# Differential attention to its output: factors and normalisation in groups of six and two heads, the root table loaded behind the last exponentials

## The chip, the cores and the metric

The kernel runs on one core of a Trainium2 chip. The metric is the device time of one execution in microseconds; a lower number is better. The engines are TensorE (PE, matrix products), VectorE (DVE), ScalarE (ACT, activation functions), GpSimd (POOL) and SyncE (SP, here the issuer of most DMAs). Each works through its own queue in order and waits on semaphores.

## The reference, cut to what matters

The program is a chain of transformer blocks on 512 tokens of width 1024: a pooling mixer with a SwiGLU, latent attention with a SwiGLU, a norm, and then one layer of a second model, differential attention followed by a mixture of 16 experts. The change is in the differential attention. The reference computes there, for 8 heads with two score maps each:

```python
q = rmsnorm(q.reshape(B, T, H, 2, dh), q_gain) * (dh ** -0.5)
k = rmsnorm(k.reshape(B, T, H, 2, dh), k_gain)
for s in range(0, T, QBLOCK):                 # 4 blocks of 128 queries
    sc = where(dist >= 0, einsum(q, k) - slopes * dist, -inf)
    p = softmax(sc, axis=-1)
    pd = p[:, :, 0] - lam * p[:, :, 1]
    outs.append(einsum('bhqk,bkhe->bqhe', pd, v))
o = rmsnorm(concatenate(outs, axis=1), subln) * (1.0 - lambda_init)
return o.reshape(B, T, H * 2 * dh) @ w_out
```

The last norm is over the 128 values of one head and one token. Then `x = x + y`, and the experts: a router picks a group and two experts in it, for each token.

## The kernel before, in words

All activations stay in SBUF as four tiles of 128 tokens (T = 4). Weights come in units of 1 MB. Each unit is split by ACT (`split_hi`, L245) and DVE (`split_lo`, L250) into a high and a low part, and a product is three matmuls (`product`, L255 to L257).

`da_attend` walks over N = H * T = 32 blocks, a block being one head and one query tile; the order is that of one loop of each engine, with block numbers that lag behind one another. For loop number i, PE makes the scores of block i + 1 (L1642), turns block i - 6 (transposes, L1653) and weighs block i - 7 with V (L1662). DVE finds the least score of block i (L1716), every fourth time makes the head's factors (L1723, L1725), and combines the two maps of block i - 6 (L1730). ACT makes the exponentials of block i with their sums in `total` (L1686), copies the turned block i - 6 to SBUF (L1694), and at i % 4 == 3 copies the finished head i // 4 - 2 to `O` (`head_out`, L1679). The maps are not divided by their sums before the weighing: `O` is left unnormalised. POOL squares each finished head but the last and folds it to 32 columns (L1750, L1752, L1755), and DVE sums those (`sum_squares`, L1705). Head 7 is squared by DVE itself in four operations (L1741).

`da_out` then makes for all 8 heads at once the factor 1 / sqrt(mean of squares / total^2 + EPS) / total: a reciprocal and a product of `total` (L1808, L1810), times the sums of squares (L1813), plus EPS (L1815), ACT's root (L1784, for which the root table is loaded at L1782), a reciprocal (L1817) and a product (L1819). Four normalisations of 128 x 1024 follow (`normal_tile`, L1799). PE turns each normalised tile with 8 transposes (L1776), ACT rounds it to the high part (L1787), and DVE takes the low part (`lo_tile`, L1804). In DVE's queue the order is normal 0, normal 1, lo 0, normal 2, lo 1, normal 3, lo 2, lo 3. PE has the transposes of all four tiles in its queue ahead of the first product with w_out, which stands in `route` (`unit_into`) and waits for `heads_lo`.

`route` adds the products to X, makes the router's logits and tables, and stores the rows. SP issues eight units of expert weights (L1886) after the last scores were read and the last head was weighed. The other 88 (L2314) wait for the routing's count and then for a free buffer. `run_experts` takes the experts one after another.

Of the kernel before, what the change touches and what calls it, by code (L numbers as in the profile page):

```python
# [32 lines left out]
ALU = mybir.AluOpType  # L33
ACT = mybir.ActivationFunctionType
AX_X = mybir.AxisListType.X

P = 128
S = 512
T = S // P
D = 1024  # L40
C = D // P
# [8 lines left out]
H = 8  # L50
# [127 lines left out]
def build_program(nc, stream, experts, x, positions, gains, rows, lams, router, consts, band, out, moe_rows):  # L178
    ctx = ExitStack()
    with ctx:  # L180
# [1160 lines left out]
        def differential_attention(block, held, w, v, down_made, mix_row_here, mix_row, mix_rows_g):  # L1341
            QT = sb("QT", [P, H, S], where=held)
            KT = sb("KT", [P, H, S], where=held)
            V = sb("da_V", [P, T, D], where=held)
            flat = sb("da_flat", [P, 2 * T * D], where=held)
            square = sb("da_square", [P, 2, 512], where=held)
            total = sb("da_total", [P, 2, H * T], where=held)
            stat = sb("da_head_stat", [P, 2, T, H], where=held)
            ls = sb("lam_s", [P, 8], where=held)
            unsloped = sb("da_unsloped", [P, H], where=held)  # L1350
            QK = flat[:, :].rearrange("p (t n) -> p t n", t=T)
            O = flat[:, T * D:2 * T * D].rearrange("p (t d) -> p t d", t=T)
            half = flat[:, 0:T * D].rearrange("p (m n) -> p m n", m=2)
            lam_ready = sem("lam_ready")
            v_here = sem("da_emptied")
            qk_here = [sem("da_qk_emptied_act"), sem("da_qk_emptied_dve")]
            scores_read = sem("d_maxed")
            heads_out = sem("d_heads_out")
            squared = sem("d_heads_squared")

            def buffer(i, m):
                h, q = divmod(i, T)
                if q < T - 1:
                    at = 768 * (h % 2) + P * q * (q + 1) // 2
                    return half[:, m, at:at + (q + 1) * P]
                if h % 2:
                    return square[:, m, :]
                return half[:, m, 1536:2048]

            da_in(block, held, w, v, down_made, mix_row_here, mix_row, mix_rows_g, QK, V, QT, KT, square, ls, unsloped, lam_ready, v_here, qk_here)  # L1370
            scored, weighed = da_attend(block, QT, KT, V, O, buffer, total, stat, ls, held, lam_ready, v_here, qk_here,
                                        scores_read, heads_out, squared)
            made, heads_lo, _ = da_out(block, O, total, stat, heads_out, squared)
            return scored, weighed, made, heads_lo


# [231 lines left out]
        def da_attend(block, QT, KT, V, O, buffer, total, stat, ls, held, lam_ready, v_here, qk_here, maxed, heads_out,  # L1608
# [10 lines left out]
            copied = sem("d_copied")  # L1619
            weighed = sem("d_weighed")  # L1620
            head_square = sem("d_head_square")
            N = H * T
            turned_probs = sb("d_turned_probs", [P, 2, S], where=held)
            least = sb("d_least", [P, 2 * N], where=held)
# [49 lines left out]

            @block.scalar
            def _(act):
                def head_out(h):
                    act.wait_ge(weighed, T * (h + 1))
                    act.activation(head_cols(h), PS[:, 6 + h % 2, :].rearrange("p (q d) -> p q d", q=T), ACT.Copy  # L1679
# [2 lines left out]
                for i in range(N + 6):  # L1682
# [13 lines left out]
                        head_out(i // T - 2)  # L1696
                    if i == 9:
                        split_hi(act, U_DA_OUT + 1)
                head_out(H - 1)

            @block.vector
            def _(dve):
# [5 lines left out]
                for i in range(N + 6):  # L1708
# [22 lines left out]
                                                 ALU.mult, ALU.add).then_inc(combined, 1)  # L1731
                    if i == 13:
                        split_lo(dve, U_DA_OUT + 1)
                    if q == 3 and h >= 3:
                        sum_squares(h - 3)
                sum_squares(H - 2)
                dve.wait_ge(heads_out, H)
                dve.wait_ge(squared, H - 1)
                last = PS[:, 6 + (H - 1) % 2, :].rearrange("p (q d) -> p q d", q=T)
                for q in range(T):  # L1740
                    dve.tensor_tensor_reduce(head_junk[:, q, :], last[:, q, :], head_cols(H - 1)[:, q, :], 1.0, 0.0,  # L1741
                                             ALU.mult, ALU.add, stat[:, 0, q, H - 1:H]).then_inc(squared, 1)

            @block.gpsimd
            def _(pool):
# [9 lines left out]
                    pool.tensor_tensor(head_junk[:, :, 0:32], head_junk[:, :, 0:32], head_junk[:, :, 32:64],  # L1755
                                       ALU.add).then_inc(head_square, 1)

            return scored, weighed


        def da_out(block, O, total, stat, heads_out, squared):
            made = sem("do_made")
            step = sem("do_step")
            rooted = sem("do_rooted")
            normal = sem("do_normal")
            heads_turned = sem("do_turned")
            heads_hi = sem("do_hi")
            heads_lo = sem("do_lo")
# [1 line left out]

            @block.tensor
            def _(pe):
                for t in range(T):
                    pe.wait_ge(normal, t + 1)
                    for c in range(C):
                        mm = pe.transpose(PS[:, 2 * t + c // 4, (c % 4) * P:(c % 4 + 1) * P],  # L1776
                                          O[:, t, c * P:(c + 1) * P], ident)
                    mm.then_inc(heads_turned, 1)

            @block.scalar  # L1780
            def _(act):
                act.activation(spare[:, 3:4], ident[:, 0:1], ACT.Sqrt).then_inc(rooted, 1)  # L1782
                act.wait_ge(step, 5)
                act.activation(stat[:, 1, :, :], stat[:, 0, :, :], ACT.Sqrt).then_inc(rooted, 1)  # L1784
                for t in range(T):
                    act.wait_ge(heads_turned, t + 1)
                    act.activation(AH[:, :, t * P:(t + 1) * P], tile_banks(t), ACT.Copy,  # L1787
# [3 lines left out]

            @block.vector
            def _(dve):
                inverse = total[:, 1, :].rearrange("p (h q) -> p q h", q=T)
                first = total[:, 0, :].rearrange("p (h q) -> p q h", q=T)

                def normal_tile(t):
                    o = O[:, t, :].rearrange("p (h d) -> p h d", h=H)
                    dve.tensor_tensor(o, o, stat[:, 1, t, :].unsqueeze(2).broadcast_to([P, H, P]),  # L1799
                                      ALU.mult).then_inc(normal, 1)  # L1800

                def lo_tile(t):
                    dve.wait_ge(heads_hi, t + 1)
                    dve.scalar_tensor_tensor(AL[:, :, t * P:(t + 1) * P], tile_banks(t), gain_col("da_sub"),  # L1804
                                             AH[:, :, t * P:(t + 1) * P].bitcast(F32), ALU.mult,
                                             ALU.subtract).then_inc(heads_lo, 1)

                dve.reciprocal(inverse, first).then_inc(step, 1)  # L1808
                dve.wait_ge(step, 1)
                dve.scalar_tensor_tensor(first, inverse, 1.0 / P, inverse, ALU.mult, ALU.mult).then_inc(step, 1)  # L1810
                dve.wait_ge(step, 2)
                dve.wait_ge(squared, H - 1 + T)
                dve.tensor_tensor(stat[:, 0, :, :], stat[:, 0, :, :], first, ALU.mult).then_inc(step, 1)  # L1813
                dve.wait_ge(step, 3)
                dve.tensor_scalar(stat[:, 0, :, :], stat[:, 0, :, :], EPS, None, ALU.add).then_inc(step, 2)  # L1815
                dve.wait_ge(rooted, 2)
                dve.reciprocal(stat[:, 0, :, :], stat[:, 1, :, :]).then_inc(step, 1)  # L1817
                dve.wait_ge(step, 6)
                dve.tensor_tensor(stat[:, 1, :, :], stat[:, 0, :, :], inverse, ALU.mult).then_inc(step, 1)  # L1819
                dve.wait_ge(step, 7)  # L1820
                normal_tile(0)
                normal_tile(1)
                lo_tile(0)
                normal_tile(2)
                lo_tile(1)
                normal_tile(3)
                lo_tile(2)
                lo_tile(3)
                for d in range(2, 4):
# [803 lines left out]
```

## Time and profile before

| | before |
|---|---|
| median of 3 runs | 1577.47 us |
| lowest and highest | 1574.33 and 1578.65 us |
| the profiled execution's own time | 1572.86 us |
| its span | 1571.0 us |
| mean granted clock of TensorE | 0.979 |
| PE busy | 1505.6 us, 96% |
| DVE busy | 779.9 us, 50% |
| ACT busy | 674.1 us, 43% |
| POOL busy | 78.9 us, 5% |

The profile is of one execution; times in it are microseconds from the start of its span. Busy shares are means over the whole span; what ends a wait in one stage is read from that stage. The granted clock is a share of 2.4 GHz: 1.00 is 2.4 GHz, 0.50 is 1.2 GHz. A line such as L255 can be that of a helper that many stages use.

### The profile page before, as it was taken

What the parts mean: (1) busy time and instruction counts of PE and PEld (TensorE: products, weight loads), DVE (VectorE), ACT (ScalarE), POOL (GpSimd) and SP (SyncE); (2) the same over time, 40 slices, a digit from 0 to 9 for tenths busy, and PEclk for the clock granted to TensorE, in tenths of its full rate; (3) what the DMA queues carried; (4) which work ended last, traced back from release to release, by engine and by line L of the source; (5) the groups of instructions that cost most, each with busy time, mean ns of one, the idle gap of its engine ahead of it and who ended that gap; (6) DMA issues with size and microseconds to landing.
All of it is one profiled execution on the core that took longest, in us unless ns stands there. A gap on an engine that the chain in (4) does not pass through costs nothing.

```text
span 1571.0 us, 19018 instructions
## 1 busy us (share of the span) xinstructions
PE 1505.6 (96%) x7399; PEld 1245.2 (79%) x7399; DVE 779.9 (50%) x941; ACT 674.1 (43%) x853; POOL 78.9 (5%) x57
## 2 busy tenths in 40 slices
PE   8899999999899999999999999999889789999996
PEld 8888888888787788888888887788557678888874
DVE  6433323232566335232332216335773679898884
ACT  5322222212355424222222124433772368777773
POOL 0000000000000000000000000000130012111210
PEclk9999999999999999999999999999998889999998
DMA  6123222232230032322223232232131379999993
GB/s 242 60 101 107 82 105 92 96 107 94 81 108 28 8 114 81 107 83 103 100 87 108 92 109 81 98 107 81 57 140 76 144 276 383 384 394 395 382 381 87
DMA packets 36207, 226.18 MB, mean 144 GB/s; under 512 B 5271, under 2 KB 5527, under 8 KB 11824
## 3 DMA queue, kind: packets, MB, share of 16 engines
q1 hardware_dynamic: 31392, 212.06, 35.9%
q0 software_dynamic: 4608, 13.22, 3.6%
q8 instruction: 45, 0.74, 0.2%
q14 instruction: 18, 0.15, 0.0%
q10 hardware_dynamic: 144, 0.03, 0.0%
HBM read 215.22 MB, written 13.63 MB: 146 GB/s over the span
## 4 chain that ended last, share of the span: by engine, by line
PE 53%; DVE 5%; DMA 3%; ACT 2%; issue 2%; DVEq 0%; ACTq 0%; SPq 0%; POOLq 0%
PE PS L255 16%; PE PS L257 16%; PE PS L256 16%; DMA eraw<-experts 3%; PE PS L1642 1%; PE PS L1662 1%; ACT WEH L2399 1%; PE PS L2332 1%; PE PS L1653 1%; DVE da_flat L1716 1%; DVE WL L250 1%; DVE WEL L2461 1%; PE PS L1982 1%; PE PS L1453 0%; PE PS L2355 0%
## 5 line engine op out<-in xcount | busy, mean ns | idle before, releaser
L250 DVE TENSOR_TENSOR WL<-raw,WH 128x2048 fp32r<-128x2048 f32 x93 | 214.0, 2301 | 432.8 <-ACT WH L245 432.8
L255 PE MATMUL PS<-AH,WL 128*128 128x512 f32 (+1 forms) x768 | 286.7, 373 | 4.3 <-DVE AL L303 4.3
L256 PE MATMUL PS<-AL,WH 128*128 128x512 f32 (+1 forms) x768 | 286.0, 372 | 0.0
L257 PE MATMUL PS<-AH,WH 128*128 128x512 f32 (+1 forms) x768 | 285.9, 372 | 0.0
L245 ACT ACTIVATE WH<-raw 128x2048 fp32r<-128x2048 f32 x93 | 177.6, 1910 | 241.2 <-PE PS L257 241.2
L2461 DVE TENSOR_TENSOR WEL<-eraw,WEH 128x2048 fp32r<-128x2048 f32 x96 | 217.3, 2287 | 21.7 <-ACT WEH L2399 21.4
L2399 ACT ACTIVATE WEH<-eraw 128x2048 fp32r<-128x2048 f32 x96 | 182.4, 1915 | 35.1 <-DMA eraw<-experts 24.5
L255 PEld LDWEIGHTS PS<-AH,WL 128*128 128x128 f32 x768 | 145.6, 190 | 29.7 <-DVE AL L303 4.5
L257 PEld LDWEIGHTS PS<-AH,WH 128*128 128x128 f32 x768 | 145.5, 189 | 25.0
L256 PEld LDWEIGHTS PS<-AL,WH 128*128 128x128 f32 x768 | 145.6, 190 | 24.8
L255 PE MATMUL PS<-WH,AL 128*128 128x512 f32 (+2 forms) x416 | 156.3, 376 | 7.7 <-DVE WL L250 7.7
L257 PE MATMUL PS<-WH,AH 128*128 128x512 f32 (+2 forms) x416 | 154.2, 371 | 0.0
L256 PE MATMUL PS<-WL,AH 128*128 128x512 f32 (+2 forms) x416 | 153.8, 370 | 0.0
L255 PE MATMUL PS<-WEH,AH 128*128 128x512 f32 x256 | 102.4, 400 | 5.7 <-DVE AH L2466 5.5
L257 PE MATMUL PS<-WEH,AH 128*128 128x512 f32 x256 | 100.4, 392 | 0.0
L256 PE MATMUL PS<-WEL,AH 128*128 128x512 f32 x256 | 100.3, 392 | 0.0
L255 PEld LDWEIGHTS PS<-WH,AL 128*128 128x128 f32 x416 | 79.4, 191 | 21.6 <-DVE WL L250 6.9
L257 PEld LDWEIGHTS PS<-WH,AH 128*128 128x128 f32 x416 | 79.3, 191 | 12.9
L256 PEld LDWEIGHTS PS<-WL,AH 128*128 128x128 f32 x416 | 79.3, 191 | 12.2
L255 PE MATMUL PS<-WH,f0FL 128*128 128x512 f32 x176 | 69.8, 396 | 0.0
L257 PE MATMUL PS<-WH,f0FH 128*128 128x512 f32 x176 | 69.6, 395 | 0.0
L256 PE MATMUL PS<-WL,f0FH 128*128 128x512 f32 x176 | 69.6, 395 | 0.0
(317 smaller groups left out, 2112.7 us busy)
## 6 DMA issues: line engine op xcount, KB each, us to landing
eraw<-experts SPq DMA_DIRECT2D x96, 1024.0 KB, 15.6
raw<-stream SPq DMA_DIRECT2D x94, 1024.0 KB, 4.8
out<-X SPq DMA_DIRECT2D x5, 512.0 KB, 2.7
moe_rows<-moe_rows_g SPq DMA_DIRECT2D x5, 512.0 KB, 2.7
X<-x SPq DMA_DIRECT2D x4, 512.0 KB, 5.4
ffn_row<-rows SPq DMA_DIRECT2D x2, 512.0 KB, 9.2
final_row<-rows SPq DMA_DIRECT2D x2, 512.0 KB, 5.9
cst<-consts SPq DMA_DIRECT2D x1, 739.5 KB, 13.6
```

The costliest lines, as they stand in the source:

```text
L245: act.activation(WH[:, u % SLOTS, :], raw[:, u % SLOTS, :], ACT.Copy).then_inc(unit_hi, 1)
L250: dve.tensor_tensor(WL[:, u % SLOTS, :], raw[:, u % SLOTS, :], WH[:, u % SLOTS, :].bitcast(F32), ALU.subtract).then_inc(unit_lo, 1)
L255: pe.matmul(acc, lhs_lo, rhs_hi, start=start, stop=False)
L256: pe.matmul(acc, lhs_hi, rhs_lo, start=False, stop=False)
L257: return pe.matmul(acc, lhs_hi, rhs_hi, start=False, stop=stop)
L1642: pe.matmul(PS[:, 2 * (i % 2) + m, 0:(q + 1) * P], QT[rows64, h, q * P:(q + 1) * P], KT[rows64, h, 0:(q + 1) * P], start=True, stop=True). ...
L1653: mm = pe.transpose(PS[:, 4 + j % 2, k * P:(k + 1) * P], buffer(j, 0)[:, k * P:(k + 1) * P], ident)
L1662: mm = pe.matmul(PS[:, 6 + h % 2, q * P:(q + 1) * P], turned_probs[:, j % 2, k * P:(k + 1) * P], V[:, k, h * P:(h + 1) * P], start=(k == 0 ...
L1716: dve.tensor_tensor_reduce(buffer(i, m), PS[:, 2 * (i % 2) + m, 0:w], const("alibi")[:, S - w:S], 2.0 ** (-8.0 * (h + 1) / H), -NEG * 1e8, ...
L1982: mm = pe.matmul(PS[:, 2 * t, 0:20], m.XT[:, t, c, :], m.wr[:, c, :], start=(c == 0), stop=(c == C - 1))
L2399: act.activation(WEH[:, k % ESLOTS, :], eraw[:, k % ERAW, :], ACT.Copy).then_inc(unit_hi, 1)
L2461: dve.tensor_tensor(WEL[:, k % ESLOTS, :], eraw[:, k % ERAW, :], WEH[:, k % ESLOTS, :].bitcast(F32), ALU.subtract).then_inc(unit_lo, 1)
```

## The change

The factors are made in two parts: heads 0 to 5 (`PARTS[0]`), and heads 6 and 7 (`PARTS[1]`). All of it moves from `da_out` into `da_attend`.

- On DVE the two operations on `total` stand in the loop at i = 35, behind combine 29. Behind the loop come the mean square of part 0, its factors, and the normalisation of tiles 0 and 1 for part 0, all ahead of the row sum of head 6 and the squares of head 7. Behind those come part 1's factors and the other six normalisations.
- The addition of EPS is dropped; it is the bias of ACT's root.
- On ACT the dummy root, which brings the table load, stands in the loop at i = 33, the root of part 0 at i = 36 (ahead of the copy of block 31), and the root of part 1 behind the copy out of head 7.
- PE's transposes are in eight groups, of 6 or 2 columns blocks, in the order of the normalisations. The first product still stands behind all of them.
- In `da_out` DVE has only the four `lo_tile` left.

```diff
@@ da_attend, scalar
+                def head_root(act, part):
+                    act.wait_ge(stepped, 3 + 2 * part)
+                    act.activation(stat[:, 1, :, PARTS[part]], stat[:, 0, :, PARTS[part]], ACT.Sqrt, bias=const("eps")
+                                   ).then_inc(rooted, 1)
...
+                    if i == N + 1:
+                        act.activation(spare[:, 3:4], ident[:, 0:1], ACT.Sqrt).then_inc(rooted, 1)
+                    if i == N + 4:
+                        head_root(act, 0)
                 head_out(H - 1)
+                head_root(act, 1)
@@ da_attend, vector
+                    if i == N + 3:
+                        dve.reciprocal(inverse, first).then_inc(stepped, 1)
+                        dve.wait_ge(stepped, 1)
+                        dve.scalar_tensor_tensor(first, inverse, 1.0 / P, inverse, ALU.mult, ALU.mult).then_inc(stepped, 1)
                     if q == 3 and h >= 3:
                         sum_squares(h - 3)
+
+                def mean_square(part):
+                    mine = PARTS[part]
+                    dve.wait_ge(stepped, 2 + 2 * part)
+                    dve.wait_ge(squared, H - 1 + T if part else H - 2)
+                    dve.tensor_tensor(stat[:, 0, :, mine], stat[:, 0, :, mine], first[:, :, mine], ALU.mult
+                                      ).then_inc(stepped, 1)
+
+                def factors(part):
+                    mine = PARTS[part]
+                    dve.wait_ge(rooted, 2 + part)
+                    dve.reciprocal(stat[:, 0, :, mine], stat[:, 1, :, mine]).then_inc(stepped, 1)
+                    dve.wait_ge(stepped, 4 + 2 * part)
+                    dve.tensor_tensor(stat[:, 1, :, mine], stat[:, 0, :, mine], inverse[:, :, mine], ALU.mult
+                                      ).then_inc(factored, 1)
+                    dve.wait_ge(factored, 2 * H + 1 + part)
+
+                def normal_part(t, part):
+                    o = O[:, t, :].rearrange("p (h d) -> p h d", h=H)[:, PARTS[part], :]
+                    size = PARTS[part].stop - PARTS[part].start
+                    dve.tensor_tensor(o, o, stat[:, 1, t, PARTS[part]].unsqueeze(2).broadcast_to([P, size, P]),
+                                      ALU.mult).then_inc(normal, 1)
+
+                mean_square(0)
+                factors(0)
+                normal_part(0, 0)
+                normal_part(1, 0)
                 sum_squares(H - 2)
...
                 # four squares of head 7
+                mean_square(1)
+                normal_part(2, 0)
+                factors(1)
+                normal_part(0, 1)
+                normal_part(1, 1)
+                normal_part(3, 0)
+                normal_part(2, 1)
+                normal_part(3, 1)
@@ da_out, tensor
-                for t in range(T):
-                    pe.wait_ge(normal, t + 1)
-                    for c in range(C):
+                for n, (t, part) in enumerate(((0, 0), (1, 0), (2, 0), (0, 1), (1, 1), (3, 0), (2, 1), (3, 1))):
+                    pe.wait_ge(normal, n + 1)
+                    for c in ((6, 7) if part else range(6)):
                         mm = pe.transpose(PS[:, 2 * t + c // 4, (c % 4) * P:(c % 4 + 1) * P],
                                           O[:, t, c * P:(c + 1) * P], ident)
-                    mm.then_inc(heads_turned, 1)
+                    if part:
+                        mm.then_inc(heads_turned, 1)
```

## Rows read from the trace of the kernel before

**Rows 1.** The page's part 4, the chain by engine, shares of the span.

```profile
PE 53%; DVE 5%; DMA 3%; ACT 2%; issue 2%; DVEq 0%; ACTq 0%; SPq 0%; POOLq 0%
```

**Rows 2.** The chain in order of time: start us, length us, what.

```profile
1173.56 0.61 ACT da_flat L1679
...
1458.52 18.95 DMA eraw<-experts
```

**Rows 3.** Timeline of PE: start, length, line, operation, count, idle before and releaser.

```profile
1186.34 1.84 PE L1776 MATMUL PS<-cst,da_flat 128*128 128x128 f32 x8 [0.36 <-DVE da_flat L1799]
1187.93 0.48 PE L255 MATMUL PS<-WH,AL 128*128 128x512 f32 x1
```

**Rows 4.** Windows: stretch, its length, busy by engine, PEclk, DMA share, GB/s.

```profile
1174.00:1178.00 4.00, 0.00 (x0) 0.00 (x0) 3.27 (x15) 1.87 (x4) 0.00 (x0) 0.96 1.01 375
1178.00:1184.00 6.00, 3.68 (x16) 3.28 (x16) 3.93 (x5) 2.23 (x2) 0.00 (x0) 0.50 1.01 423
1184.00:1188.00 4.00, 3.63 (x17) 3.23 (x17) 3.12 (x3) 1.11 (x1) 0.00 (x0) 0.51 0.31 129
1280.00:1450.00 170.00, 170.00 (x810) 141.37 (x810) 152.90 (x88) 135.28 (x96) 35.07 (x18) 1.00 1.01 385
```

**Rows 5.** Timeline of SP, the issues of expert weights.

```profile
1163.31 12.29 SPq L1886 DMA_DIRECT2D eraw<-experts  x8
...
1263.25 263.61 SPq L2314 DMA_DIRECT2D eraw<-experts  x88
```

**Rows 6.** Timeline of DVE, combines 30 and 31, squares, factors, normalisation, low parts.

```profile
1169.35 0.60 DVE L1730 SCALAR_TENSOR_TENSOR da_flat<-da_flat,d_factor 128x384 f32<-128x384 f32 x1
1169.88 0.74 DVE L1730 SCALAR_TENSOR_TENSOR da_square<-da_square,d_factor 128x512 f32<-128x512 f32 x1
...
1174.19 0.29 DVE L1741 CUSTOM_DVE_ANT_0 d_head_junk<-PS,da_flat 128x128 f32<-128x128 f32 x1 [0.45 <-ACT da_flat L1679]
...
1175.04 0.35 DVE L1808 RECIPROCAL da_total<-da_total 128x32 f32<-128x32 f32 x1
...
1177.11 2.36 DVE L1799 TENSOR_TENSOR da_flat<-da_flat,da_head_stat 128x1024 f32<-128x1024 f32 x2
1181.54 1.28 DVE L1804 SCALAR_TENSOR_TENSOR AL<-PS,gain,AH 128x1024 fp32r<-128x1024 f32 x1 [2.07 <-ACT AH L1787]
1182.74 1.22 DVE L1799 TENSOR_TENSOR da_flat<-da_flat,da_head_stat 128x1024 f32<-128x1024 f32 x1
```

**Rows 7.** Timeline of ACT's copies and table load, and of PE behind the copies.

```profile
1167.34 0.60 ACT L1694 ACTIVATE d_turned_probs<-PS 128x512 f32<-128x512 f32 x1 [0.39 <-PE PS L1653]
1168.98 0.28 ACT L1694 ACTIVATE d_turned_probs<-PS 128x128 f32<-128x128 f32 x1 [1.05 <-PE PS L1653]
1169.89 0.39 PE L1662 MATMUL PS<-da_V,d_turned_probs 128*128 128x128 f32 x2
...
1174.18 1.28 ACT L1782 ACT_TABLE_LOAD   x1
1175.47 0.20 ACT L1782 ACTIVATE spare<-cst 128x1 f32<-128x1 f32 x1
```

**Rows 8.** Timeline of DVE's factor operation without and with POOL beside it.

```profile
1162.16 0.22 DVE L1725 SCALAR_TENSOR_TENSOR d_factor<-d_factor,lam_s,da_total 128x4 f32<-128x4 f32 x1
...
1166.57 1.04 POOL L1750 TENSOR_TENSOR d_head_junk<-da_flat 128x512 f32<-128x512 f32 x1 [4.64 <-ACT da_flat L1679]
1166.60 1.03 DVE L1725 SCALAR_TENSOR_TENSOR d_factor<-d_factor,lam_s,da_total 128x4 f32<-128x4 f32 x1
...
1171.04 1.04 POOL L1750 TENSOR_TENSOR d_head_junk<-da_flat 128x512 f32<-128x512 f32 x1 [2.09 <-ACT da_flat L1679]
```

**Rows 9.** Windows of other stretches, for the granted clock (columns as in rows 4).

```profile
966.00:970.00 4.00, 4.00 (x12) 3.15 (x11) 4.00 (x3) 2.78 (x6) 0.00 (x0) 0.57 0.78 266
1132.00:1134.00 2.00, 0.17 (x2) 0.00 (x0) 1.93 (x9) 1.13 (x4) 1.41 (x2) 1.00 0.48 70
1243.00:1269.00 26.00, 13.06 (x53) 11.82 (x53) 17.24 (x53) 12.29 (x12) 4.19 (x3) 0.50 0.40 145
```

More of the change, by code:

```diff
@@ L1370, in differential_attention @@
             da_in(block, held, w, v, down_made, mix_row_here, mix_row, mix_rows_g, QK, V, QT, KT, square, ls, unsloped, lam_ready, v_here, qk_here)
-            scored, weighed = da_attend(block, QT, KT, V, O, buffer, total, stat, ls, held, lam_ready, v_here, qk_here,
+            scored, weighed, normal = da_attend(block, QT, KT, V, O, buffer, total, stat, ls, held, lam_ready, v_here, qk_here,
                                         scores_read, heads_out, squared)
-            made, heads_lo, _ = da_out(block, O, total, stat, heads_out, squared)
+            made, heads_lo, _ = da_out(block, O, normal)
             return scored, weighed, made, heads_lo
@@ L1621, in da_attend @@
             head_square = sem("d_head_square")
+            stepped = sem("d_stat_step")
+            rooted = sem("d_rooted")
+            normal = sem("d_normal")
+            PARTS = (slice(0, H - 2), slice(H - 2, H))
+            inverse = total[:, 1, :].rearrange("p (h q) -> p q h", q=T)
+            first = total[:, 0, :].rearrange("p (h q) -> p q h", q=T)
             N = H * T
@@ L1756, in _, with da_out @@
                                        ALU.add).then_inc(head_square, 1)
-            return scored, weighed
-        def da_out(block, O, total, stat, heads_out, squared):
+            return scored, weighed, normal
+        def da_out(block, O, normal):
             made = sem("do_made")
-            step = sem("do_step")
-            rooted = sem("do_rooted")
-            normal = sem("do_normal")
             heads_turned = sem("do_turned")
@@ L1772, in _ @@
             def _(pe):
-                for t in range(T):
-                    pe.wait_ge(normal, t + 1)
-                    for c in range(C):
+                for n, (t, part) in enumerate(((0, 0), (1, 0), (2, 0), (0, 1), (1, 1), (3, 0), (2, 1), (3, 1))):
+                    pe.wait_ge(normal, n + 1)
+                    for c in ((6, 7) if part else range(6)):
                         mm = pe.transpose(PS[:, 2 * t + c // 4, (c % 4) * P:(c % 4 + 1) * P],
                                           O[:, t, c * P:(c + 1) * P], ident)
-                    mm.then_inc(heads_turned, 1)
+                    if part:
+                        mm.then_inc(heads_turned, 1)
             @block.scalar
             def _(act):
-                act.activation(spare[:, 3:4], ident[:, 0:1], ACT.Sqrt).then_inc(rooted, 1)
-                act.wait_ge(step, 5)
-                act.activation(stat[:, 1, :, :], stat[:, 0, :, :], ACT.Sqrt).then_inc(rooted, 1)
                 for t in range(T):
@@ L1793, in _ @@
             def _(dve):
[L1794 to L1800, printed above, removed]
                 def lo_tile(t):
@@ L1806, in lo_tile @@
                                              ALU.subtract).then_inc(heads_lo, 1)
[L1808 to L1822, printed above, removed]
                 lo_tile(0)
-                normal_tile(2)
                 lo_tile(1)
-                normal_tile(3)
                 lo_tile(2)
```

## The prediction

> **What bounds the kernel now.** I read the page's chain first, by engine: TensorE (PE) holds 53% of the span and every other engine a few per cent [rows 1], so a change on VectorE (DVE) counts only where PE stands still for it. The chain in order of time shows where: the last head's weighed sum is copied out from 1173.56 [rows 2], and the first product with w_out starts at 1187.93 [rows 3]. In these 14.4 us single steps of DVE, ScalarE (ACT) and PE take turns: squares of head 7, factor steps to 1177.11, then tile by tile normalise, transpose, round, take the rest. PE has all four tiles' transposes ahead of the first product, so the last normalisation and its eight transposes (from 1186.34, 1.84 us) stand in series before it.
>
> The windows add the clock [rows 4]: 0.96 on average in 1174 to 1178, where PE does nothing, and 0.50 (1.2 GHz) until just before the products; a transpose then takes 0.23 us.
>
> What follows shifts as a block. The expert weights have eight buffers, filled by eight issues from 1163.31; the other 88 issues start at 1263.25 [rows 5], behind the routing, which is behind these products. From there the DMA is busy all the time (share 1.01, 385 GB/s, [rows 4]), and the end of the chain waits for it, 18.95 us in one piece [rows 2]. A stream that starts x earlier ends x earlier, and nothing of it can start before the routing has counted its rounds. So a microsecond saved ahead of 1187.93 is worth one at the end.
>
> **The change, step by step.** I take the times of the profiled run and play the new order of each queue against them.
>
> (a) Two small operations on `total`, a reciprocal (0.35) and the product of inverses (as 1162.16, 0.22), move in front of the row sum of head 5 and combines 30 and 31, at i = 35 on DVE [rows 6, 8]. Combine 30 (1169.35, 0.60) then ends at 1170.5 instead of 1169.95, combine 31 at 1171.2. PE turned block 30 right behind the matmuls of 1169.89 [rows 7], at about 1170.3; now it can't before 1170.55. I charge 0.3 us on the attention's last blocks.
>
> (b) The root table load goes to ACT at i = 33, behind the copy that starts at 1167.34 and ends at 1167.94. It costs 1.28 and its dummy root 0.20 [rows 7]. The copy for block 28 starts at 1169.4 instead of 1168.98 and ends at 1169.7; PE needs it for the matmuls of 1169.89. Hidden, with 0.2 to spare, at no cost; with that cover gone it costs up to 1.5. The Trainium skill, page "ScalarE: Activation LUTs", section "What ACT_TABLE_LOAD costs", adds some 1.38 us of drain to a load of 1.28; by it the copy would end at 1171.1 and the last head come about 1.1 us later than in my sum. The trace disagrees: the load at 1174.18 starts 0.02 behind the copy before it, and its own activation 1.29 later.
>
> (c) `head_root(0)` stands on ACT ahead of copy 31 and waits for DVE's mean square of heads 0 to 5. Behind it are queued copy 31, for which PE's last weighed sum waits, and head 7's copy out, for which DVE's squares wait. The mean square comes behind combine 31 (1171.2), just when GpSimd (POOL) squares head 6 (1171.04, 1.04 us). What that can do is in [rows 8]: DVE's factor operation takes 0.22 at 1162.16, and 1.03 at 1166.60 beside the same POOL square. Both read two SBUF tiles, as the mean square does. Bounds: nothing, if POOL's square is the one that waits, to 1.0 us. I take that POOL goes first: mean square ends 1172.25, root 1172.5, copy 31 ends 1173.1, the last sum 1174.3, and head 7 is in SBUF at 1174.95 instead of 1174.16: 0.8 later, the 0.3 of (a) included.
>
> (d) Meanwhile DVE does factors(0) and two normalisations of six heads. A tile of 1024 columns takes 1.14 from start to start (2.36 for two, less the last one's 1.22), and 384 columns take 0.60 where 1024 take 1.22 [rows 6]: 0.97 ns a column, so 768 columns cost 0.89 and 256 columns 0.39. Reciprocal and product (0.47), and at most 0.3 of waiting for each of POOL's last two operations, put the first normalisation at 1173.4 and the end of the second at 1175.2. With the row sum of head 6 it is 1175.4. Head 7 has been there since 1174.95: from here DVE is the chain.
>
> (e) From 1175.4 DVE does: four squares, 0.85 (1174.19 to 1175.04); mean square 0.25; tile 2 of six heads 0.89, under which ACT's second root disappears; reciprocal and product 0.47; two tiles of two heads 0.79; tile 3 of six 0.89; two of two 0.79. That is 4.93, to 1180.3. Then the first lo tile, 1.20 start to start (1181.54 to 1182.74), to 1181.5. Its inputs are there: the last transposes of tile 0 go at about 1178.4, and ACT's rounding (1.1) is over by 1179.9. Product at 1181.55. The other lo tiles end 1.2 apart and PE takes 12 x 0.227 = 2.7 a tile, so they are hidden. Eight normalisations instead of four cost 4 x 0.08 = 0.3, in that sum; the addition of EPS is gone into the root's bias.
>
> (f) Clock. PE no longer stands still for 4.9 us; its longest gap is some 1.3. But behind 1174.3 it has only 12 transposes (1.3 us at full clock) in three microseconds. Rows for both sides [rows 9]: 1.00 in 1132 to 1134 with PE busy 0.17 of 2; 0.57 in 966 to 970 with PE busy throughout. If the clock falls near 1177.7, the remaining 20 transposes take 4.6 us, the first product starts at 1182.3, and PE works without a break before it, as from 1184 on, where the clock then rose. Bounds: nothing; 0.7 if it rises before the products; 2.4 if 3.4 us of products run cold (4 us at a mean of 0.57 are 3.4 us at 0.50), half of which is lost. I take 0.3, between the first two.
>
> Sum: 1187.93 - 1181.55 = 6.4, less 0.3 is 6.1; 6.0 with a few new semaphore waits of some 0.03. The ends are 7.4 (POOL waits, no clock loss) and 4.0. The profiled run took 1572.86 us with a span of 1571.0, so it would take 1566.9. The median of the timed runs is 1577.47, 4.6 above that run; for the median I forecast 1571.5.
>
> **Rivals.**
> 1. The clock falls and the products start cold: 0.7 + 1.7, gain 4.0, time 1573.5. For it: products did run cold in 966 to 970 [rows 9], and six-head bursts are thin work. Against it: 1184 to 1188 [rows 4], where PE had little but sixteen transposes, and the mean of 0.51 is 0.50 with the rise at the very end, just before the first product. The Trainium skill, page "TensorE: Matmul & The Clock Gate", Part 4 "PE-mode transpose", says that transposes don't count as PE-busy; by it the clock would fall and rise well inside the products, which is this rival. The trace speaks against the rule with that 0.51. 25%.
> 2. ACT's new load and root hold up the last blocks more than I charge: copy 28 misses its slot, or the mean square waits for all of POOL's three operations (to 1173.4). Head 7 comes at 1176.3 and DVE waits 0.9 for it: gain 5.1, with both 4.5; time 1572.7. For it: 1.03 instead of 0.22 [rows 8]. Against it: POOL's three wait for one another, and DVE can go in between. 10%.
> 3. The block doesn't shift whole: the thin work of the routing meets the clock otherwise, or the expert stream gives the time back. For it: 26 us of the routing at 0.50 [rows 9], so the clock there is at the edge. Against it: the stream is the end, and starts from the routing alone. Gain 1, time 1576.5. 8%.
> 4. Slower: the clock falls at about 1177.7 and stays at 1.2 GHz under the products, as it stayed in 1243 to 1269 [rows 9]. A product matmul then takes twice its 0.227, so half of the cold time is lost; the gain of 6.4 is gone after 12.8 us of it, and with 20 us the kernel is 3.6 slower, 1581. Against it: PE works without a break there, as from 966 on, where most of the 4 us were cold but not all. 4%.
>
> **Numbers.** Forecast 53%, with 1570 to 1573.2 as its own range; rivals 25, 10, 8 and 4%. A measurement of this kernel can tell about 0.3% (4.7 us) from no change. The forecast (gain 5 to 7.4, and medians spread a microsecond or so) gives faster in some 0.85 of its cases, rival 1 in a third, rival 2 in half, which with rounding is 0.60; 0.05 slower, the rest the same. The range takes in rivals 1 and 2 and, with a microsecond of spread, both ends of the sum, and leaves out the last two: 1568 to 1576.
>
> **What would show it.** In the changed kernel's trace: the first product at 1181 to 1182.5, and the 88 issues from about 1257; the table load behind block 27's copy, and block 28's copy still ahead of its matmuls; head 7's copy out at about 1174.4, because ACT's root waited for a mean square as long as POOL's square; DVE without a gap from head 6's row sum to the first lo tile; the clock low under transposes at most. I am wrong if the products start after 1183, if DVE waits for head 7, if products run at 0.43 each, or if the stream's start moves and the end doesn't.

## The result, and the profile after

The changed kernel took 1566.38 us (median of 5 runs, 1565.85 to 1571.12). The kernel before took 1574.83 us in the same measurement (median of 5, 1574.33 to 1578.65). The ratio is 0.9948, with a 95% interval of 0.9928 to 0.9968: faster by half a per cent, 8.2 us. Forecast were 1571.5 us and a gain of 6.0. The time is 5.1 us below the forecast and 1.6 us below its stated range; the gain was forecast 2.2 us smaller than this measurement has it.

Two more measurements of the changed kernel, described below, gave ratios of 0.9958 and 0.9949. Over all three, 21 runs of it have a mean of 1568.3 us; 83 runs of the kernel before, in three later measurements, have one of 1575.6 (standard deviation of a single run 2.3 and 3.4). The difference is 7.3 us, with some 1.2 us of uncertainty from the spread of the runs; how far measurements differ beyond that is shown below. One execution of a version below (late table) took 3868.05 us, at a clock of 1.00, and is left out of its mean and ratio.

The profiled execution took 1566.38 us, with a span of 1564.6. PE in order of time (start, length, line, operation, count, idle before; L1828 is the old L1776):

```profile
1173.62 0.88 PE L1828 MATMUL PS<-cst,da_flat 128*128 128x128 f32 x6
1174.76 0.87 PE L1828 MATMUL PS<-cst,da_flat 128*128 128x128 f32 x6 [0.26 <-DVE da_flat L1776]
1177.17 4.10 PE L1828 MATMUL PS<-cst,da_flat 128*128 128x128 f32 x20 [1.54 <-DVE da_flat L1776]
1181.54 0.47 PE L255 MATMUL PS<-WH,AL 128*128 128x512 f32 x1 [0.27 <-DVE AL L1846]
```

The last line is the number the forecast turned on: the first product starts at 1181.54, where it started at 1187.93 [rows 3] and 1181.55 was worked out before the clock's 0.3. This trace reached the stage 0.21 earlier than the one before did (combine of block 28 at 1167.45 against 1167.66); without that it is 1181.75, against 1181.95 with the clock and the semaphore waits in. DVE, and then ACT, in the same stretch:

```profile
1170.17 0.74 DVE L1746 SCALAR_TENSOR_TENSOR da_square<-da_square,d_factor 128x512 f32<-128x512 f32 x1
1170.84 0.19 DVE L1761 TENSOR_TENSOR da_head_stat<-da_head_stat,da_total 128x24 f32<-128x24 f32 x1
1172.19 2.51 DVE L1776 TENSOR_TENSOR da_flat<-da_flat,da_head_stat 128x768 f32<-128x768 f32 x2
1175.04 0.29 DVE L1788 CUSTOM_DVE_ANT_0 d_head_junk<-PS,da_flat 128x128 f32<-128x128 f32 x1
1177.47 2.30 DVE L1776 TENSOR_TENSOR da_flat<-da_flat,da_head_stat 128x256 f32<-128x256 f32 x5
1180.11 4.86 DVE L1846 SCALAR_TENSOR_TENSOR AL<-PS,gain,AH 128x1024 fp32r<-128x1024 f32 x4 [0.34 <-ACT AH L1837]
```

```profile
1167.74 1.28 ACT L1711 ACT_TABLE_LOAD   x1
1169.03 0.20 ACT L1711 ACTIVATE spare<-cst 128x1 f32<-128x1 f32 x1
1169.14 0.26 ACT L1705 ACTIVATE d_turned_probs<-PS 128x128 f32<-128x128 f32 x1
1173.62 0.60 ACT L1690 ACTIVATE da_flat<-PS 128x512 f32<-128x512 f32 x1 [1.25 <-PE PS L1668]
```

The mean square (1170.84) takes 0.19 and not 1.0. The two normalisations ahead of head 7's squares (1172.19) take 2.51 together, the five behind them (1177.47) run without a gap, and lo tile 0 waits 0.34 for ACT. The table load (1167.74) holds up block 28's copy: against [rows 7] that starts 0.16 later, in a trace that is 0.21 earlier as a whole, so by 0.37. The matmuls that read it still start in their old place, 0.21 earlier (1169.68 for 1169.89): the delay is hidden.

The windows (columns as in rows 4) and SP's issues:

```profile
1174.00:1178.00 4.00, 2.20 (x16) 1.73 (x15) 3.68 (x16) 0.52 (x2) 0.00 (x0) 0.93 0.93 363
1178.00:1181.00 3.00, 3.00 (x17) 2.80 (x15) 2.66 (x5) 2.04 (x2) 0.00 (x0) 0.52 1.01 410
1181.00:1184.00 3.00, 2.73 (x14) 2.10 (x13) 3.00 (x4) 2.20 (x3) 0.00 (x0) 1.00 1.02 429
1280.00:1450.00 170.00, 170.00 (x808) 141.45 (x808) 153.75 (x88) 136.73 (x97) 35.91 (x19) 1.00 1.02 389
```

```profile
1163.10 13.13 SPq L1911 DMA_DIRECT2D eraw<-experts  x8
1257.50 264.16 SPq L2339 DMA_DIRECT2D eraw<-experts  x88
```

The clock fell near 1177.4 and was back ahead of the products. The stream of the 88 issues starts 5.75 us earlier than in [rows 5]: 0.64 of the 6.4 went in the routing. Its thin matmuls (PE waits for DVE, then 32 of 20 columns) stand in the chain of waits after with

```profile
1234.02 5.23 PE PS L2007 x32
...
1471.66 19.02 DMA eraw<-experts
```

where the chain of the kernel before, in the same place, has

```profile
1240.39 4.61 PE PS L1982 x32
```

The low clock reaches more of them now: 0.50 on average in 1236 to 1240 here, 1.00 in the same window of before and 0.57 in 1242 to 1246, where the same matmuls stand there. The stream, from its first issue to the end of the span, took 307.10 us instead of 307.75 and gave that back. The sum, before less after: 0.21 ahead of block 28's combine, -0.27 in the last blocks, 6.45 from head 7's copy out to the first product, -0.64 in the routing, 0.65 in the stream, together 6.4. The last term is chance: the stream took 304.9 to 311.0 us in the 13 traces of this document, and 307.0 to 309.6 in the three of the changed kernel.

### The profile page after: what moved, and what is told of

It reads as the page before. It is cut to its first block, busy times and chain, and to the rows that moved or that the text cites. A ratio compares the mean times of both kernels' runs of the same rounds, so it can differ in the third digit from the quotient of the medians.

```text
span 1564.6 us, 19025 instructions
## 1 busy us (share of the span) xinstructions
PE 1504.3 (96%) x7399; PEld 1244.3 (80%) x7399; DVE 780.5 (50%) x947; ACT 673.8 (43%) x854; POOL 79.5 (5%) x57
## 4 chain that ended last, share of the span: by engine, by line
PE 53%; DVE 5%; DMA 3%; issue 2%; ACT 2%; DVEq 0%; ACTq 0%; SPq 0%; POOLq 0%
PE PS L255 16%; PE PS L257 16%; PE PS L256 16%; DMA eraw<-experts 3%; PE PS L1648 1%; PE PS L2357 1%; DVE da_flat L1732 1%; PE PS L1659 1%; DVE WL L250 1%; PE PS L2007 1%; ACT WEH L2424 1%; PE PS L1668 1%; PE PS L1453 0%; DVE da_flat L1746 0%; DVE WEL L2486 0%
```

## The experiments

All were run on one core; each measurement of several kernels shares its runs of the kernel before. Since the 13 traces reach this stage up to 4 us apart (below), the stage is read by the distance between two of its own events: from the start of head 7's copy out to the first product, 14.37 us before (1173.56 to 1187.93) and 7.92 after (1173.62 to 1181.54).

The second column is from one trace of each version. Where a kernel was traced more than once, it came to 14.37 and 14.31 (before), and to 7.92, 7.49 and 8.11 (change); so a difference under 0.6 between two versions means something only where the clock did the same in both. The means are over 12, 8, 12, 12, 12, 6, 11, 8, 8, 6 and 8 runs, from the top. Diffs are cut to the lines that matter, and `@@` names the engine.

| kernel | copy out to product, us | ratio to before, 95% interval | mean of its runs, us |
|---|---|---|---|
| before, again | 14.31 | 1.0023 (1.0006 to 1.0041) | 1578.1 |
| change, again | 7.49 | 0.9958 (0.9941 to 0.9974) | 1568.8 |
| order only | 11.12 | 0.9987 (0.9973 to 1.0001) | 1572.8 |
| early steps | 13.68 | 0.9991 (0.9976 to 1.0005) | 1574.8 |
| before, PE filled | 12.77 | 0.9994 (0.9977 to 1.0011) | 1573.3 |
| change, no POOL on head 6 | 6.81 | 0.9939 (0.9920 to 0.9958) | 1565.7 |
| change, late table | 11.81 | 0.9985 (0.9971 to 0.9999) | 1573.2 |
| change, tile first | 8.11 | 0.9955 (0.9938 to 0.9971) | 1568.7 |
| all three remedies | 6.59 | 0.9956 (0.9938 to 0.9973) | 1567.8 |
| change, PE filled | 7.48 | 0.9945 (0.9927 to 0.9964) | 1566.8 |
| change, third time | 8.11 | 0.9949 (0.9929 to 0.9970) | 1568.0 |

The kernel before against itself gave 1.0023, an interval that leaves out 1. A ratio here is thus no better than 0.2 to 0.3%, and differences between two versions are read from the second column.

### Both kernels again

No edit.

> The kernel before, unchanged, to see how its executions spread. The change gained 6.4 us between two profiled executions but 8.4 us between medians. Theory C (clock): executions differ in when TensorE's clock falls and rises, so a run with a mean granted clock lower by 0.002 has some 6 us more at 1.2 GHz and takes 2 to 4 us longer; the profiled execution of before (1572.86 us, clock 0.979) had the clock back just at its first product, at 1187.9, and most others have it back later. Then the runs here spread over 1573 to 1579 in a few steps, and the first product of this trace runs partly at 0.43 us a matmul. Rival N (chance): the runs spread evenly with no tie to the clock, and the first product starts at 1187.9 at full clock again, with a time near 1575.

> The changed kernel, unchanged, beside the one before on the same chip. Theory C: again 8 us (ratio 0.9948, +-0.001) between the medians, and the first product at 1181.5 with a full clock, because the clock's low stretch is over under the transposes whatever its position. Rival N: the 8.4 was chance; the ratio comes to 0.9960 (6.4 us).

The runs of the kernel before spread over 1571 to 1584, and those beside them over 1569 to 1580. Longer runs go with a lower mean clock: of the 83, the 13 with 0.980 have a mean of 1571.5, the 20 with 0.979 one of 1573.3, the 14 with 0.978 1575.2, and the 17 with 0.976 1578.5; of the 21 of the changed kernel, those with 0.982 1566.6 and those with 0.979 1570.5. The other part of theory C fell: in the second trace of before the first product ran at full clock too. The changed kernel's second ratio, 0.9958, is what rival N said (0.9960), but its interval takes in theory C's 0.9948 too. The spread comes from elsewhere, ahead of this stage and behind it, in code that no version here changed. The windows of the kernel before [rows 9] have 0.57 in 966 to 970; those of the changed kernel, second time:

```profile
962.00:966.00 4.00, 2.10 (x10) 1.44 (x9) 3.96 (x4) 2.59 (x4) 0.00 (x0) 1.00 0.08 16
966.00:970.00 4.00, 4.00 (x19) 3.32 (x18) 3.96 (x5) 2.78 (x6) 0.00 (x0) 1.00 0.69 250
```

What that is worth is seen between two reciprocals of the same code. DVE in the kernel before:

```profile
958.33 0.16 DVE L277 RECIPROCAL rstd<-rstd 128x1 f32<-128x1 f32 x1 [1.55 <-ACT rstd L708]
...
979.00 0.16 DVE L277 RECIPROCAL rstd<-rstd 128x1 f32<-128x1 f32 x1
```

and in the changed kernel, second time:

```profile
957.66 0.16 DVE L277 RECIPROCAL rstd<-rstd 128x1 f32<-128x1 f32 x1 [1.54 <-ACT rstd L708]
...
976.73 0.16 DVE L277 RECIPROCAL rstd<-rstd 128x1 f32<-128x1 f32 x1
```

20.67 us against 19.07: one low stretch costs 1.6 us here. The same execution of the changed kernel then had a low stretch where the one before had none:

```profile
1132.00:1136.00 4.00, 2.06 (x18) 1.61 (x16) 3.90 (x15) 2.83 (x8) 1.41 (x2) 1.00 0.69 223
1132.00:1136.00 4.00, 4.00 (x21) 2.92 (x20) 2.40 (x11) 3.04 (x10) 0.38 (x1) 0.57 0.61 240
```

The first is the kernel before; between two reciprocals around it DVE took 14.01 us there (1133.24 to 1147.25) and 15.78 in the second (1130.74 to 1146.52), so the 1.6 were lost again. Block 28's combine started anywhere from 1166.70 to 1170.72 in the 13 traces, with hardly a difference in the code before it.

### The order alone, and the early steps alone

```diff
                 normal_tile(0)
                 normal_tile(1)
-                lo_tile(0)
                 normal_tile(2)
-                lo_tile(1)
                 normal_tile(3)
+                lo_tile(0)
+                lo_tile(1)
                 lo_tile(2)
```

> The kernel before with one thing changed: in DVE's queue the four normalisations stand ahead of the four lo tiles; no groups, nothing earlier. Theory A (the order is most of it): the normalisations end at 1181.8, PE has its last transposes done by 1184.4, lo tile 0 ends at 1183; the first product starts near 1184.4 instead of 1187.9, 3.5 us or more of the change's 6.4. Theory B (the work done ahead of the last head is most of it): PE's cold transposes (0.23 each, 32 of them from 1178.4) or the lo tiles hold it up, and the product starts at 1186 or later, under 2 us of gain.

The product came 11.12 us behind the copy out, 3.2 us earlier than before: theory A, with 3.5 expected. The four normalisations run on, and PE turns all four tiles in one piece of 6.54 us at 0.2 us each; PE, mostly at 1.2 GHz (0.50 in 1178 to 1181), is the limit, since the product follows its last transpose at once and lo tile 0 was over at 1181.96:

```profile
1177.42 6.54 PE L1776 MATMUL PS<-cst,da_flat 128*128 128x128 f32 x32 [4.86 <-DVE da_flat L1799]
1183.71 0.48 PE L255 MATMUL PS<-WH,AL 128*128 128x512 f32 x1
```

The second kernel keeps the table load, the two operations on `total` and EPS where the change puts them, but makes one group of 8 heads, in the old queues. The lines of DVE are told in words here.

```diff
                 head_out(H - 1)
-                head_root(act, 1)
+                act.activation(stat[:, 1, :, :], stat[:, 0, :, :], ACT.Sqrt, bias=const("eps"))
@@ vector: no parts; behind the squares of head 7
+                tensor_tensor, reciprocal, tensor_tensor on all 8 heads
+                normal_tile(0), normal_tile(1), lo_tile(0), normal_tile(2), ...
```

> The changed kernel without its groups: the table load at i = 33, the two operations on total at i = 35 and EPS in the root's bias stay, but the factors are made for all 8 heads at once behind the last squares, and the queues of DVE and PE are as before (normal 0, 1, lo 0, normal 2, lo 1, ...). Theory A and B both: 0.35 + 0.2 + 0.3 us are gone from the chain, 0.3 comes back from the later combines; the first normalisation starts at 1176.5 instead of 1177.1 and the first product at 1187.3, 0.6 us of gain. Rival T (the table load behind the last exponentials matters): 1.3 us or more.

13.68, 0.7 earlier than before, 0.6 expected. Rival T fell: with one group, ACT's table load was no part of the chain, and moving it alone is worth little.

### What the early table load is worth

```diff
-                    if i == N + 1:
-                        act.activation(spare[:, 3:4], ident[:, 0:1], ACT.Sqrt).then_inc(rooted, 1)
-                    if i == N + 4:
-                        head_root(act, 0)
                 head_out(H - 1)
+                act.activation(spare[:, 3:4], ident[:, 0:1], ACT.Sqrt).then_inc(rooted, 1)
+                head_root(act, 0)
```

> The changed kernel with the root table loaded where it was before, behind head 7's copy out, and the root of part 0 behind it; groups and orders stay. It measures what the early load is worth. Theory: the root of part 0 is over at 1.49 + 0.6 + 0.3 = 2.4 us behind the start of head 7's copy, the two normalisations that stood ahead of the squares come behind that, and the first product is 1.8 (two normalisations) + 2.4 - 1.0 later: 10.5 to 11 us behind head 7's copy out instead of 7.9, so the early load carries some 3 us of the gain. Rival: DVE's chain has slack, and the product comes less than 1.5 us later.

11.81, 3.9 later than with the change and 0.8 more than the 10.5 to 11 expected; lo tile 0 waited 0.56 for ACT (0.34 in the changed kernel), beside transposes at 1.2 GHz (0.50 in 1184 to 1188). DVE, with the mean square of part 0 long done, waits 4.94 us for the root, and everything of head 7 stands behind it:

```profile
1174.10 0.21 DVE L1759 TENSOR_TENSOR da_head_stat<-da_head_stat,da_total 128x24 f32<-128x24 f32 x1
1179.24 0.30 DVE L1765 RECIPROCAL da_head_stat<-da_head_stat 128x24 f32<-128x24 f32 x1 [4.94 <-ACT da_head_stat L1685]
1179.82 1.83 DVE L1774 TENSOR_TENSOR da_flat<-da_flat,da_head_stat 128x768 f32<-128x768 f32 x2
```

So the early load carries all that the groups bring: with a late one the kernel comes out 0.7 behind the order alone (11.12), by one trace of each. And without the groups the load is worth nothing that shows (13.68). The two normalisations take 1.83 here, where POOL is idle.

### POOL beside the first normalisations

```diff
-                sum_squares(H - 2)
+                dve.tensor_reduce(stat[:, 0, :, H - 2], head_junk[:, :, 0:32], AX_X, ALU.add).then_inc(squared, 1)
@@ gpsimd
-                for h in range(H - 1):
+                for h in range(H - 2):
```

> The changed kernel without POOL's three operations on head 6, so head 6's sums of squares are left out (the row sum is still taken, of old data). It measures what POOL costs DVE in the new place. Theory L (two engines, one way to SBUF): the two six-head normalisations of tiles 0 and 1 take 1.8 together instead of 2.5, the row sum follows at once, and the mean square and everything else of DVE up to the squares of head 7 is 0.7 to 0.9 earlier; but head 7's copy out is the limit then, so the first product is 0.4 to 0.8 us earlier, 7.1 us behind the copy. Rival: the 2.5 us are the normalisation's own, and nothing moves.

This kernel leaves out head 6's squares, so it is a measurement and no version to use. As theory L had it: DVE's pair takes 1.83 instead of 2.51, and the product comes at 6.81 instead of 7.49, in two traces with the clock at 1.00. The pair in this kernel, and POOL in the changed one:

```profile
1171.68 1.83 DVE L1776 TENSOR_TENSOR da_flat<-da_flat,da_head_stat 128x768 f32<-128x768 f32 x2
```

```profile
1170.83 1.10 POOL L1805 TENSOR_TENSOR d_head_junk<-da_flat 128x512 f32<-128x512 f32 x1 [2.10 <-ACT da_flat L1690]
1172.01 0.74 POOL L1807 TENSOR_TENSOR d_head_junk<-d_head_junk 128x256 f32<-128x256 f32 x1
1172.83 1.05 POOL L1810 TENSOR_TENSOR d_head_junk<-d_head_junk 128x128 f32<-128x128 f32 x1
```

POOL's last operation, 0.45 alone, takes 1.05 too: each waits for the other in turn. The Trainium skill, page "SBUF — State Buffer", section "Who interferes with whom", says that a VectorE instruction with two SBUF inputs contends with a GpSimd instruction that reads SBUF, and that the port pair they share is an exclusive lock; the 0.68 and the 0.60 agree.

### The low clock

Matmuls that nobody reads keep PE at work in its gaps: in the kernel before 19 behind the last weighed sum and 9 ahead of tile 2, in the changed one 5 behind the transposes of tile 1's first six heads.

```diff
+                def keep_busy(bank, count):
+                    for _ in range(count):
+                        pe.matmul(PS[:, bank, :], WH[:, u0 % SLOTS, 0:P], WH[:, u0 % SLOTS, 0:512], start=True, stop=True)
+                pe.wait_ge(unit_lo, u0 + 2)
+                keep_busy(3, 19)
                 for t in range(T):
+                    if t == 2:
+                        keep_busy(7, 9)
                     pe.wait_ge(normal, t + 1)
```

> The kernel before, with PE kept at work in its two gaps: 19 matmuls of 512 columns into a free PSUM bank behind the last weighed sum, and 9 ahead of tile 2's transposes; nobody reads them. It measures what the low clock cost before. Theory C: the clock stays 1.00 through 1174 to 1190, transposes take 0.11 us instead of 0.23, the first product comes 12.5 us behind head 7's copy out instead of 14.35 (two times 0.9 us on the chain), and the timed runs, whose clock is 0.977 in the mean against 0.979 of the profiled one, gain more than that: 3 us or more, with mean clocks of 0.981 and above. Rival N (the spread is not from here): the trace gains 1.8 us and the timed runs gain 1.8 too, with the spread as before.

> The changed kernel with the five filling matmuls alone. In one profiled execution of the changed kernel the clock fell under the transposes and the first product came 7.92 us behind head 7's copy out, in another it did not and it came 7.49. Theory: the fill makes it 7.5 every time, 0.4 us at most. Rival: the five matmuls delay the transposes of tile 2, and it is 7.9 or later.

Before: 12.77, 1.5 to 1.6 earlier, and the windows show 1.00 throughout:

```profile
1174.00:1178.00 4.00, 4.00 (x22) 3.46 (x23) 2.11 (x13) 2.29 (x4) 0.90 (x2) 1.00 1.00 360
1178.00:1184.00 6.00, 5.42 (x32) 4.15 (x30) 4.68 (x6) 2.25 (x3) 0.00 (x0) 1.00 1.00 415
```

The timed runs gained 2.1 us in the mean, with a standard error of 1.1 (the ratio, 0.9994, has about 1). That doesn't tell theory C's 3 from rival N's 1.8. The mean clock rose from 0.978 to 0.981, some 10 us less at 1.2 GHz, for 1.5 to 1.6 us of this stage: only the transposes that ACT and DVE waited for lengthen it. After: 7.48, as in the trace in which the clock stayed up by itself (7.49). The fill cost nothing in that trace; by the traces in which the clock fell (7.92 and 8.11) it can be worth 0.4 to 0.6, but with one trace it isn't shown that it was the fill that kept the clock up.

### Toward a better version

First only the order. In DVE's queue lo tile 0 stands ahead of normal(2, 1) and lo tile 1 ahead of normal(3, 1); PE's transposes of these two stand behind the first products of tile 0 and of tile 1.

```diff
                 lo_tile(0)
+                normal_part(dve, 2, 1)
                 lo_tile(1)
+                normal_part(dve, 3, 1)
@@ route, tensor
                         mm = unit_into(d, t)
+                        if d == 0 and t < 2:
+                            turn_late(pe, 6 + t)
```

> The changed kernel, with lo tile 0 ahead of the last two normalisations of two heads in DVE's queue, and PE's transposes of those behind the first product of tile 0 and of tile 1. If DVE's queue is what the first product waits for, it comes 0.7 us earlier, 7.1 us behind head 7's copy out, and the kernel is 0.7 us faster than the changed one. If cold transposes and ACT's rounding hold it (the changed kernel's lo tile 0 waited 0.34 us for ACT), it comes 0.3 us earlier at most.

8.11: nothing gained at the first product. The clock fell near 1178.7 in this trace, and lo tile 0 waited 1.21 us for ACT, which waited for cold transposes:

```profile
1181.77 1.28 DVE L1852 SCALAR_TENSOR_TENSOR AL<-PS,gain,AH 128x1024 fp32r<-128x1024 f32 x1 [1.21 <-ACT AH L1843]
```

Behind it the trace has something that a reading by the first product misses: the 88 issues start 82.93 us behind head 7's copy out, against 83.41 to 84.39 in the changed kernel's three traces. The routing took 74.82 from the first product on, not 75.92 to 76.28, with its thin matmuls at full clock (1.00 in 1236 to 1240). Whether the order does that, or where the clock's low stretch happened to fall, is open; the timed mean, 1568.7, has no gain.

Then all three: this order, the five filling matmuls, and head 6 squared by DVE out of PSUM while it would wait for the root of part 0.

```diff
                 mean_square(0)
+                squares_here(H - 2)
                 factors(0)
                 normal_part(dve, 0, 0)
                 normal_part(dve, 1, 0)
-                sum_squares(H - 2)
@@ gpsimd
-                for h in range(H - 1):
+                for h in range(H - 2):
```

> A version built from what the runs showed: DVE squares head 6 itself out of PSUM, in the time in which it waits for the root of part 0, so POOL has nothing beside the normalisations; lo tile 0 stands ahead of the last two small normalisations, and their transposes behind products; five matmuls nobody reads keep PE at work between tile 1's and tile 2's transposes. If the three costs add (0.7 of POOL, 0.4 of cold transposes, 0.7 of DVE's queue), the first product is 6.1 to 6.3 us behind head 7's copy out instead of 7.5 to 7.9, and the kernel is 1.5 us faster than the changed one. If ACT's rounding or head 7's copy is the limit, 6.8 and under 1 us.

> The changed kernel once more, for the pair with the one before and with the two above on the same chip. If the gain is the 6.4 to 6.8 us of this stage, the ratio is 0.9957 to 0.9960; the first 8.4 us were then the spread of medians of five.

6.59, 0.9 to 1.5 earlier than the changed kernel (7.49, 7.92, 8.11). Against 7.49, the trace with the clock up as here, it is 0.9, of which leaving POOL out had 0.68 alone. The costs did not add to 6.1: lo tile 0 still waited 0.48 for ACT. The timed runs, 1567.8 against 1568.0 of the changed kernel beside it with errors of 0.8 and 0.6, can't tell the two apart. The third time of the changed kernel gave 0.9949: the stage's 6.4 to 6.8 us (0.9957 to 0.9960) lie inside its interval, and so does the first measurement's 8.2 (0.9948), so it doesn't settle which it is.

## Why the prediction was right and wrong

**What follows shifts as a block.** Held in the main, and the exact match is luck: 6.4 us at the first product were 6.4 at the end of the span, because 0.64 lost in the routing met 0.65 found in a stream whose length differs by more from trace to trace. The loss in the routing is in all three traces of the change: 75.92 to 76.28 us from the first product to the 88 issues, against 75.32 and 75.38. The prediction put it at nothing; rival 3 named the mechanism, with a far larger price.

**(a) and (b).** Block 30's turn came late as said, and from block 28's combine to head 7's copy out it was 6.17 instead of 5.90: 0.27, where 0.3 was charged. The table load was hidden; it held block 28's copy up by 0.37, where 0.42 was worked out. Its dummy root began 1.29 behind the load's start here too, so the drain weighed there did not show.

**(c) failed, at no cost to the sum.** POOL did not go first: the mean square took 0.19 and POOL's square 1.10, so the 0.5 beyond (a) were not lost. Head 7's copy out came at 1173.62 and not at the 1174.4 named as a sign. The contention came with the next DVE operations of two SBUF inputs that met POOL, the normalisations.

**(d)** had the normalisations at 0.89 each, 1.78 the pair, which is right without POOL (1.83), and up to 0.6 of waits ahead of them. In fact they started 1.2 earlier than said (1172.19; 1.0 without this trace's 0.21), took 2.51, and head 7's squares began at 1175.04 instead of 1175.4 (0.15 earlier without the 0.21). The errors of (c) and (d), -1.0 and +0.7, and 0.2 at the row sum nearly cancelled: luck, not a right sum.

**(e)** From the squares to lo tile 0: 4.93 were worked out, 5.07 measured, of them 0.34 of waiting for ACT; from there to the product 1.43, not 1.25. The order by itself brought 3.2 us and the early steps 0.7. The other 2.5 to 3 are, by subtraction, the groups with the table load ahead of them. The prediction gave no such split; it would have shown that the plainest edit, four lines in another order, is half of the change.

**(f)** The clock fell in two of three traces of the changed kernel, and under transposes only: 0.4 to 0.6, with 0.3 taken and a bound of 0.7. Rival 1 did not happen. In 1178 to 1181 the clock came back with nothing but transposes on PE (0.52 in that window, then 1.00), as in [rows 4]. By the Trainium skill, page "TensorE: Matmul & The Clock Gate", Part 4, they should not count; this trace too speaks against that.

**The step that failed** is the last: "The median of the timed runs is 1577.47, 4.6 above that run; for the median I forecast 1571.5", with "medians spread a microsecond or so". The same sum put the profiled run at 1566.9, and it took 1566.38. The base was wrong: five runs of the kernel before, those three among them, have a median of 1574.83. That is 2.6 of the 5.1 us by which 1571.5 was off; the range laid around that base would have begun at 1565.4. The other 2.4 are the gain between the medians, 8.45 for 6.0, which the trace (6.4) has only 0.4 of. Medians of the same kernel came to 1577.47 (3 runs), 1574.83 (5), 1575.69 (31), 1578.44 (12), 1575.45 (25) and 1574.56 (15): they spread by 3.9 us, and a single run has a standard deviation of 3.4. With the 83 runs' mean of 1575.6 as its base the same gain gives 1569.6. The median of five measured first, 1566.38, was a low one in its turn, 1.9 under the mean of the 21. The range should have been some 2 us wider on either side for that alone. A low clock stands at six places of the trace of before (from 40, 416, 966, 1177, 1242 and 1550 us on); the prediction weighed two of them, this stage's and the routing's, and gave the spread nothing for the rest.

What stays open: the timed gain, 7.3 us, is 1.4 above the mean difference of the profiled executions (two spans of before, 1571.0 and 1570.7; three after, 1564.6, 1563.5 and 1566.9: 5.9 us). The timed one is uncertain by some 1.2 and the one of five traces by more, so they may be the same. Whether timed runs of the kernel before pay more at this stage than its two traces show was not seen, since those runs have no traces.

## What to carry to other kernels

When small steps of several engines take turns, first try the queue order alone: all of one kind ahead of the next engine's dependants gave half of the stage's gain here. Splitting a reduction in parts pays only if everything the early part needs (a table load above all) is moved with it: late, it cost 3.9 us of 6.5, and the parts then brought nothing over the order alone. Judge a gain under 1% by the distance between two events of the stage in several traces; and base an absolute forecast on the spread of many runs, not on the median of three.

## What the runs showed of the hardware

The same pause of PE can be followed by a low clock or not. Ahead of the products at 966 PE stood idle for 1.90 us in both traces:

```profile
965.63 0.47 PE L255 MATMUL PS<-WH,AL 128*128 128x512 f32 x1 [1.90 <-DVE WL L250]
964.96 0.47 PE L255 MATMUL PS<-WH,AL 128*128 128x512 f32 x1 [1.90 <-DVE WL L250]
```

In the kernel before (first line) the clock was 0.57 in 966 to 970, in the changed kernel's second trace 1.00, and that was 1.6 us. Over whole runs of the kernel before, means go from 1571.5 us at a clock of 0.980 to 1578.5 at 0.976. Five 512-column matmuls that nobody reads, in a pause of PE, cost nothing in time (7.48 against 7.49), and the clock was 1.00 behind them; it was so in two traces without them too. And VectorE instructions of two SBUF operands and a GpSimd one beside them lost 0.6 to 0.7 us to each other.
